# Fills of the expert rows in memory: issued beside the second layer's z products, not in the first layer's mLSTM

## What is computed

```python
def _token_mixers(h, l, hist, p):
    z = h @ p['w_in'][l]
    mq, mk, mv, mo, mi, mf, aq, ak, av, iq, ik, iw, pu = jnp.split(z, _split_points(), axis=-1)
    ...  # mLSTM (4 heads) | attention over keys that an indexer selects (8 heads) | causal pooling
```

```python
    dots = jnp.einsum('bqjd,bsd->bqjs', q_idx, k_idx).astype(f32) * D_IDX ** -0.5
    score = jnp.einsum('bqj,bqjs->bqs', w_idx.astype(f32), jax.nn.relu(dots))
```

## Time and profile before

| | us |
|---|---|
| median of 3 runs | 2233.93 |
| the runs | 2231.75, 2233.93, 2235.88 |
| the profiled execution | 2235.12 |
| its span, first to last instruction | 2233.4 |
| PE busy | 2063.2 (92%) |
| DVE, ACT, POOL busy | 1308.9, 996.8, 181.5 |

### The profile page before, as it was taken

One profiled execution on the slowest core, in us unless ns is written; L12 is line 12 of the kernel. 1 busy time (PEld: TensorE's weight loads), 2 busy tenths in 40 slices (PEclk: granted clock), 3 DMA queues, 4 the chain that ended last, 5 costly groups with the idle time before them and its releaser, 6 DMA issues.

```text
span 2233.4 us, 36658 instructions
## 1 busy us (share of the span) xinstructions
PE 2063.2 (92%) x14266; PEld 1708.0 (76%) x14292; DVE 1308.9 (59%) x2052; ACT 996.8 (45%) x1456; POOL 181.5 (8%) x271
## 2 busy tenths in 40 slices
PE   6999878898999999998998788979899999999996
PEld 4999745588999999998997445966566657788883
DVE  2657654354544545456477553555565657789884
ACT  5522125444423443435211264435444556677772
POOL 3000120110000000000000111111010010000201
PEclk7999769999999999999997699978999999999998
DMA  9222668533545454642223357126677788899994
GB/s 328 65 76 76 162 189 292 183 122 95 167 126 165 136 157 132 172 126 78 61 73 85 89 190 239 47 93 236 202 262 233 242 271 311 327 372 373 375 382 179
DMA packets 272094, 418.23 MB, mean 187 GB/s; under 512 B 21214, under 2 KB 216312, under 8 KB 271952
## 3 DMA queue, kind: packets, MB, share of 16 engines
q1 hardware_dynamic: 249984, 349.50, 47.1%
q0 software_dynamic: 21968, 66.72, 9.2%
HBM read 385.73 MB, written 29.59 MB: 186 GB/s over the span
## 4 chain that ended last, share of the span: by engine, by line
PE 84%; DVE 5%; ACT 4%; DMA 3%; issue 2%; POOL 0%; ACTq 0%; PEldq 0%; DVEq 0%; PEld 0%; POOLq 0%; SPq 0%
PE banks L941 80%; PE banks L945 4%; DVE scratch L2522 1%; ACT scratch L1887 1%; DMA weight_ring<-in_w_ada 1%; DVE region L2522 1%; ACT hidden_t L1887 1%; ACT region_split L1887 1%; DMA scratch<-bias_rows 1%; ACT region L1887 0%; DVE weights_lower L2522 0%; DMA hidden_t<-h_rows,pass_tokens 0%; ACTq L1902 0%; DMA region<-in_pool_scale 0%; DMA expert_ring<-in_we 0%
## 5 line engine op out<-in xcount | busy, mean ns | idle before, releaser
L941 PE MATMUL banks<-upper_parts,region_split 128*128 128x320 f32 x1664 | 390.2, 310 | 4.5 <-DVE upper_parts L2522 4.5
L941 PE MATMUL banks<-upper_parts,weights_lower 128*128 128x320 f32 (+1 forms) x1248 | 387.1, 310 | 0.0
L2522 DVE TENSOR_TENSOR expert_lower<-expert_ring,region_split 128x1408 fp32r<-128x1408 f32 (+1 forms) x198 | 286.1, 1469 | 103.7 <-PE banks L941 78.3
L941 PE MATMUL banks<-region_split 128*128 128x320 f32 (+1 forms) x1264 | 342.1, 333 | 3.0 <-DVE upper_parts L2522 3.0
L941 PEld LDWEIGHTS banks<-upper_parts,region_split 128*128 128x128 f32 x1664 | 284.5, 189 | 4.8 <-issue 4.8
L1887 ACT ACTIVATE region_split<-expert_ring 128x1408 fp32r<-128x1408 f32 (+1 forms) x198 | 241.6, 1256 | 57.8 <-DMA expert_ring<-in_we 45.4
L941 PEld LDWEIGHTS banks<-region_split 128*128 128x128 f32 x1264 | 223.0, 188 | 25.0 <-issue 8.4
L941 PEld LDWEIGHTS banks<-upper_parts,weights_lower 128*128 128x128 f32 (+1 forms) x1248 | 235.3, 189 | 0.0
L941 PE MATMUL banks<-region_split,upper_parts 128*128 128x384 f32 x732 | 234.3, 385 | 0.0
L2522 DVE TENSOR_TENSOR weights_lower<-weight_ring,region_split 128x2048 fp32r<-128x2048 f32 (+2 forms) x72 | 168.9, 2350 | 96.2 <-ACT region_split L1887 96.2
L1887 ACT ACTIVATE region_split<-weight_ring 128x2048 fp32r<-128x2048 f32 (+2 forms) x72 | 140.6, 1958 | 164.2 <-PE banks L941 162.5
(11 more groups left out here) (333 smaller groups left out, 3276.1 us busy)
## 6 DMA issues: line engine op xcount, KB each, us to landing
expert_ring<-in_we SPq DMA_DIRECT2D x176, 704.0 KB, 6.3
expert_ring<-in_we SPq DMA_DIRECT2D x121, 512.0 KB, 4.3
weight_ring<-in_w_ada SPq DMA_DIRECT2D x48, 1024.0 KB, 9.3
weight_ring<-in_w SPq DMA_DIRECT2D x88, 512.0 KB, 4.8
weight_ring<-in_w_in SPq DMA_DIRECT2D x24, 1024.0 KB, 5.3
weight_ring<-in_w SPq DMA_DIRECT2D x16, 1408.0 KB, 6.2
weight_ring<-in_w_out SPq DMA_DIRECT2D x8, 1024.0 KB, 6.9
y_rows<-residual_t POOLq DMA_DIRECT2D x4, 1760.0 KB, 23.6
```

What stands on the lines that cost most here:

```text
L941: return nc.tensor.matmul(out, lhsT, rhs, start=first, stop=last)
L2522: return v.tensor_tensor(out, x, y, op)
```

## The change

The six fills move from the first layer's mLSTM to the head of the second layer's stage z: POOL waits for the end of `ffn0` and issues them ahead of the copy of the doubled keys. The waits for their end move from behind `mlstm0` to behind `mlstm1`. The source is `XT` as before.

```diff
             for l in range(DEPTH):
+                if l % 2:
+                    after(f"ffn{l - 1}")
+                    spare = d["y_rows"][LEAST_PASSES * PASS:, :].rearrange("(r t p) n -> r p t n", r=4, t=4)
+                    filler = XT[0:spare.shape[1], :, :].rearrange("p k t -> p (k t)")[:, 0:4 * D].rearrange("p (t n) -> p t n", n=D)
+                    load(spare_filled, *((spare[r, :, :, :], filler) for r in range(3)))
+                    seats = d["y_rows"][0:LEAST_PASSES * PASS, :].rearrange("(i p) n -> p i n", p=PASS)[P:, :, :]
+                    load(spare_filled, *((seats[:, at:at + 4, :], filler[0:RIDERS, :, :]) for at in (0, 4)))
+                    load(rider_y_out, (spare[3, :, :, :], filler))
                 pool.wait_ge(gate_rows_used, l + 1)
                 load(keys_twice, (IK[HD:P, :], IK[0:HD, :]))
                 after(f"z{l}")
...
                 load(kidx_in, (KIC[:, :, 0, :], kidx), (KIC[:, :, 1, :], kidx))
-                if l == 0:
-                    spare = d["y_rows"][LEAST_PASSES * PASS:, :].rearrange("(r t p) n -> r p t n", r=4, t=4)
-                    filler = XT[0:spare.shape[1], :, :].rearrange("p k t -> p (k t)")[:, 0:4 * D].rearrange("p (t n) -> p t n", n=D)
-                    load(spare_filled, *((spare[r, :, :, :], filler) for r in range(3)))
-                    seats = d["y_rows"][0:LEAST_PASSES * PASS, :].rearrange("(i p) n -> p i n", p=PASS)[P:, :, :]
-                    load(spare_filled, *((seats[:, at:at + 4, :], filler[0:RIDERS, :, :]) for at in (0, 4)))
-                    load(rider_y_out, (spare[3, :, :, :], filler))
                 after(f"mlstm{l}")
...
                 pool.wait_ge(state_out, STATE_OUTS * (l + 1))
-                if l == 0:
+                if l % 2:
                     pool.wait_ge(spare_filled, 80)
                     pool.wait_ge(rider_y_out, 16)
                 after(f"index{l}")
```

## The result

The changed kernel takes 2247.64 us, the median of four runs (2241.97, 2247.63, 2247.64, 2247.75). The kernel before took 2233.59 beside it (four runs, 2231.75 to 2235.88). The ratio is 1.0057, with a 95% interval of 1.004 to 1.0074: slower, by more than the 0.2% that a measurement here can tell from no change. The forecast of 2233.7 with a range up to 2237.9 was wrong. Run again, unaltered, it gave 1.0068 (1.0042 to 1.0095).

A forecast was written before the change was run, and what follows sets the result against it. PE was taken to bound the kernel. From the unchanged median of 2233.93 us, 0.26 was subtracted for the first mLSTM, with 0 for the issue and 0 for waits: 2233.7 us, range 2231.8 to 2237.9.

The forecast's parts named there:

- What bounds the kernel: Whole kernel: 84% of the last-ending chain is PE, so a change counts only where PE waits, in z in full.
- The gain of the removal, -0.26: First layer's mLSTM: without the fills it shortens from 57.75 to 57.49 us, by the issue's delay of DVE.
- The issue at the head of z at nothing: Head of second z: POOL's 4.53 us of issuing delays DVE's steps by 0, at most 0.3 us.
- The keys behind the fills: Second z: doubled keys queue behind 8.3 MB of fills and land at 1054.1, before PE needs them at 1055.12.
- the long end: Fills' own time in POOL's queue, upper estimate: 40.9 us, ending at 1053.5; the middle taken was 37.5.
- the short end: Fills' own time in POOL's queue, lower estimate: 34.1 us, counted from the landing of the last load ahead, ending at 1046.7.
- The clock after the wait, at most 1.7: Second z after a long wait: PE's dense work runs 3.3 us at half speed, costing about 1.7 us.
- If that entry is there, its length is the whole cost: Sign in PE's waits in z: an entry for region<-region lengthens the second z by just its length.
- a short wait: Rival in second z: keys land at 1055.1 to 1059.3, PE waits up to 4.2 us; at most 2237.9 us; chance 0.31.
- The weight chunk, cover of 18.9 us: Second z: the chunk loaded at 1031.36 costs nothing, because ACT first reads it 18.9 us after its landing.
- the prediction's rival it landed at 1058.8: Rival in second z: the weight chunk waits for all fills, yet PE doesn't wait; 2233.7 us; no separate chance given.
- The long wait: Rival in second z: PE waits up to 5.5 us for the keys and the clock may fall; 2238.4 to 2240.9; chance 0.11.

The follow-up runs named there:

- keys first: The changed kernel, but POOL copies the doubled keys before it waits for the end of ffn0 and issues the six fills; 2234.85 us, ratio 1.0011.
- the six with spread sources: The changed kernel, but the two small fills read every fourth partition instead of the first 32; 2235.19 us, ratio 0.9993.
- the shorter rows: The changed kernel, but with each fill cut into four of 256 columns, 24 transfers in place of 6; 2243.67 us, ratio 1.0053.
- keys from another queue: The changed kernel, but ACT instead of POOL issues the copy of the doubled keys, in both layers; 2234.93 us, ratio 1.0009.
- the two alone: The changed kernel with the four large fills left in mlstm0, small ones at the head of z: from neighbouring partitions 2231.63 us, spread out 2237.23.

## Why the prediction was wrong, point by point

**What bounds the kernel: right.** A wait of PE in z counts in full. 8.2 us of wait and what the clock adds are the 10.99 us by which z is longer.

**The gain of the removal, -0.26: fell.** The first mLSTM takes 57.75 to 57.80 us in seven of the twelve profiles, with all six fills in it (before), with some (two kernels) or with none (the changed kernel, "keys first", the six with spread sources, the shorter rows), and 57.48 in "keys from another queue". In the other four it takes 58.15 to 59.29, at a mean granted clock of 0.54 to 0.56 instead of 0.59. So nothing was gained, and what the stage's length goes with is the clock.

The 0.32 us for 0.23 that DVE's copy takes at the stage's head was read wrongly. It is not POOL's issue of the fills but that of the index keys' loads, which stays. POOL's and DVE's timelines of the changed kernel, then of its second run:

```profile
248.37 2.39 POOL L697 DMA_DIRECT2D hidden_t<-in_cache_kidx  x2
250.49 0.32 DVE L2520 COPY scratch<-region 128x128 f32<-128x128 f32 x1
...
247.58 2.39 POOL L697 DMA_DIRECT2D hidden_t<-in_cache_kidx  x2
250.08 0.23 DVE L2520 COPY scratch<-region 128x128 f32<-128x128 f32 x1
```

In the first POOL issues until 250.76 and the copy starts 0.27 us before that; in the second POOL is through at 249.97, 0.11 us before the copy. In eight profiles, that of before among them, the copy starts 2.12 or 2.13 us after the start of this issue and takes 0.31 to 0.33 us; in a ninth it starts 0.13 us before the issue's end and takes 0.23. No such copy without an issue of POOL beside it took more than 0.23; beside an issue of fills it took 0.54, 0.26 and 0.23 in three kernels. This agrees in kind with what the Trainium skill says in SBUF — State Buffer, section "Who interferes with whom", as the prediction has it, but the fills had no part in it here. The pair was no pair of twins either: in the first layer POOL also issues the loads of the gates ahead of the index keys (`vectors_t`, 1.7 us in the changed kernel), so its issue there reaches until 5.6 us after the stage's start, in the second layer until 4.0, and the copy comes at 5.4. And one pair of stages is no measurement of a quarter of a microsecond.

**The issue at the head of z at nothing: right.** 4.50 us of POOL, and PE's wait for `hidden_lower_parts` is 4.1 before and after. (The text ahead of the prediction says that POOL waits nowhere else for stages. It does, at every `after(...)` of its program, as the diff shows for `z`, `mlstm` and `index`; the change isn't touched by this.)

**The keys behind the fills: the right mechanism, the wrong size. This is the step that failed.** The prediction named this term as the one that decides, and gave the rival for it. It put the keys' landing 43.3 us after the fills' first issue (1054.1 - 1010.8), at most 49.8, and the measured distance is 52.2 (1058.05 - 1005.86). PE was to have 1.0 us in hand; it waited 8.2. Two sizes in the sum failed.

First, how the transfers share the engines: I took 3 us for the chunks, because they would pass beside idle engines of the fills' tail. The queues by stretches show what happened (packets, MB, share of 16 engines; q0 is POOL's, q1 SP's). The changed kernel from its first bytes for 30 us, then the last 12.1 us before the last fill's landing, and then the last 12.1 us of the fills before the change, in the first mLSTM:

```profile
q0 software_dynamic: 2373, 6.96, 91.5%
q1 hardware_dynamic: 504, 0.51, 4.9%
...
q1 hardware_dynamic: 1507, 1.52, 38.0%
q0 software_dynamic: 144, 0.55, 13.1%
...
q0 software_dynamic: 346, 1.02, 24.9%
```

For 30 us the fills are as fast beside z as they were beside the mLSTM: 6.96 of their 8.3 MB are through at 1037.7, where the old place had moved 7.63 MB in as long, some 1 MB of them index keys. Then 1.3 MB need another 20 us. In its last 12.1 us q0 moves 0.55 MB instead of 1.02, half the pace, while q1 moves 1.52 MB, and the two together fill only 51% of the engines. q0's 13.1% are the time of two engines of the 16. I read this so: most engines had no fill left and the few that had one were shared, so the chunks did not pass beside the tail, they stretched it. No run takes the chunks away, so this reading is not tested by itself. Over 1027 to 1053 us the whole came to 203 GB/s, where the old place made 254 and a chunk 346:

```profile
DMA packets 3106, 5.29 MB, mean 203 GB/s; under 512 B 330, under 2 KB 2329, under 8 KB 3103
```

By the sum's own terms it is 51.7 - 1.8 = 49.9 us from the first bytes to the last fill, so 9.0 us for the chunks if the fills' own time is the long end's 40.9, where I took 3 and at most 6.1. The 6.1 was no bound: it priced the chunks by their bytes at the pace of 16 engines, and counted two of them, while SP issued a third at 1047.38, before the last fill had landed. That it is so few engines that hold the end is read from the shares; which ones, and how many, the rows used here don't say.

Second, the fills' own time, where I took the middle of 34.1 and 40.9 us, and their shape. In the second mLSTM, beside one chunk instead of three, they took 44.3 us from the first issue. Measured as the short end was, from the landing of the last load of index keys (1200.9 + 8.4 = 1209.3) to that of the last fill (1246.4), it is 37.1 us, where the old place had 34.1. That is 3 us for one chunk, and the 9.0 above would be 3 for each of three. An estimate from single profiles, then: of the 9.4 us by which the fills' end was missed (49.9 for 37.5 + 3), 6.0 are the chunks' and 3.4 the fills' own time; the runs don't separate the two any better. The prediction also held against the small size of the Trainium skill's formula that "the first fill alone took 17.7 us". That fill had the index keys ahead of it in the queue; in the changed kernel, with nothing ahead, the first one landed 12.2 us after its issue. The last landing, 46.7 us and here 51.7, speaks as plainly against the estimate of 21 us.

Nothing in the prediction asked who makes the tail. The issues of the first mLSTM say it, one by one: 17.7, 21.6 and 25.6 us to landing for the first three large fills, 4 us apart, then 29.6 and 37.2 for the two small ones. Each small fill has 0.29 of the bytes of a large one; the second of them took 7.6 us more than the first. With them away the last fill landed 38.5 us after the first's issue, with their source spread out 42.1, and in both the wait is gone.

**The clock after the wait, at most 1.7: 2.8.** It was at 0.50 from 1058 to about 1064, 6 us and not the 3.3 us that I had carried over from the head of z. z lost 2.3 us beyond the wait of 6.3 in the second run, 1.7 beyond 4.1 with one large fill kept back, and 2.2 beyond 2.4 with the shorter rows (167.21 - 162.62 - 2.42). Of the last, these stretches show the clock's fall behind the wait of 1049.65 to 1052.07:

```profile
1050.00:1052.00 2.00, 0.00 (x0) 0.00 (x0) 0.00 (x0) 0.13 (x2) 0.00 (x0) 1.00 1.06 327
1052.00:1054.00 2.00, 1.93 (x14) 1.63 (x15) 0.10 (x1) 1.98 (x2) 0.00 (x0) 0.93 0.72 250
1054.00:1056.00 2.00, 2.00 (x11) 2.00 (x11) 2.00 (x1) 1.88 (x4) 0.00 (x0) 0.50 0.26 91
```

"If that entry is there, its length is the whole cost" was wrong each time. So a short wait would have cost some 2 us more than the prediction's rival of that name, which left the clock out, allowed for.

**The weight chunk, cover of 18.9 us: enough for PE, not for ACT.** It landed in 28.9 us instead of 5.3 (the row of 5.3 is that of the chunk of 1038.4; this one had taken 5.2). ACT, which had 18.9 us to spare, waited for it 4.63:

```profile
1055.12 1.91 ACT L1888 ACTIVATE z_weights_upper<-weight_ring 128x2048 fp32r<-128x2048 f32 x1 [4.63 <-DMA weight_ring<-in_w_in]
```

In the prediction's rival it landed at 1058.8, 27.4 us after the issue, and PE was not to wait. Size and verdict were right: in the two kernels that take the keys out from behind the fills, ACT waited 2.95 and 4.38 us for chunks of 32.1 and 28.6 us, and PE nothing.

**The second mLSTM, 1.1 us longer: not foreseen, settled in part.** Without a wait in z, and without fills in this stage, it took 57.47 to 57.50 us in all seven profiles, that of before among them. With one it took 58.61 in the changed kernel, 58.96 in its second run, 59.09 with one large fill kept back, and 56.90 with the shorter rows, where the wait was shortest. So a wait in z disturbs the stage behind it, mostly but not always to its loss. In the second run what is longer is the clock's doing, 0.54 instead of 0.58, with PE busy for 49.10 us instead of 46.45 for as many products, and so it is with the large fill kept back (0.54, 49.21):

```profile
1206.57:1265.53 58.96, 49.10 (x272) 31.11 (x273) 37.33 (x93) 12.02 (x33) 3.95 (x4) 0.54 0.20 45
```

In the changed kernel the clock is 0.58 as before, but PE's wait for DVE's `mix_t` is 3.2 us instead of 1.2, and 1.0 in the other two. Why DVE is late there was not tried.

**The chances.** The long wait had 0.11, with at most 2240.9. By the profile it deserved more: the sum had 1.0 us in hand between terms that were known to 6.8 (the fills) and 6.1 us (the chunks), and its long ends came out together, because, by the reading above, the chunks weigh on the same few engines that make the fills long. The lower bound of 2231.8 by a scatter of 2 us was too narrow as well; the kernel before alone spread over 15 us in 26 runs.

## What to carry to other kernels

A short transfer on which an engine waits must not stand behind long ones in the same queue: issued first, or from another queue, it was in time here, and the megabytes beside it cost nothing that could be measured. When a queue's drain decides, price other traffic against the slow tail and not against the mean pace, look at how each source lies across the partitions, and when a margin is smaller than the spread of its terms, give the wait an even chance. A saving that rests on one pair of stages and is under half a microsecond is none until several executions show it.

## What the hardware showed that was not expected

- A transfer of 32 x 4 x 1024 floats from the first 32 partitions to memory moved some 203 GB/s, from every fourth partition 346; the same 288 packets took 1.75 times as long. The Trainium skill, SBUF — State Buffer, section "Door 1: The DMA port swizzle", has a rule for it: the pace depends on how many of the 16 DMA ports the partitions reach, and partitions 0 to 31 reach only half. The traces agree in kind; by the number of ports the ratio would be 2, and they show 1.7.
- Spreading them brought the last landing of the six forward by 9.6 us (8.0 against the second run), four times the 2.3 us that it brought the two alone.
- The first weight chunk of 1 MB that SP loaded beside the fills took 26.1 to 32.1 us (five profiles with all six fills and the one with five; 22.8 with the small ones spread, 19.0 without them), 5.3 alone, and a copy of 160 KB 12.6 us from ACT's queue, 4.7 alone, and 23.5 behind the fills in theirs.
- A pause of PE of 2.4 us in z was followed by a granted clock of 0.50, though only 1.7 us after PE had started again, and for some 3 us; in the pause of 8.2 us it fell after the first four, and it stayed low for six more when PE had started again. z lost 1.7 to 2.8 us beyond the wait itself.
- DVE's copy of 128 x 128 took 0.31 to 0.33 us where it began some 0.25 us before the end of POOL's issue of two loads (eight profiles) and 0.23 wherever POOL issued nothing, once 0.54 beside the issue of the fills.
